# Two-layer decoder trunk in fp32 on one core: work reordered at the second mixer's entry and behind the last expert, the last gate product cut in two, decay logits in rounded parts

## The chip, the core and the metric

The kernel runs on one core of one Trainium2 chip. The metric is device time in microseconds of one execution. The engines are TensorE (PE), VectorE (DVE), ScalarE (ACT), GpSimd (POOL) and SyncE (SP); each works through its own instructions in order, and waits on semaphores tie them together.

## What is computed

A causal decoder trunk of two layers on 256 tokens of width 1024, all fp32:

```
for i in range(2):
    u = rmsnorm(h, mix_norm_gain[i])
    fq, fk, fv, fg, hq, hf, hi, hg = split(u @ w_in[i])
    a = head_rmsnorm(forgetting_attention(fq, fk, fv, fg, bias[i]))
    r = head_rmsnorm(hgrn2_recurrence(hq, hf, hi, lower_bounds[i])) * silu(hg)
    h = h + concat(a, r) @ w_out[i]
    u = rmsnorm(h, ffn_norm_gain[i])
    h = h + (swiglu(u) if i == 0 else moe_swiglu(u))      # top 2 of 8 experts
    u = rmsnorm(h, ple_norm_gain[i])
    h = h + (p[i] @ w_ple[i]) * sigmoid(u @ w_ple_gate[i])
return rmsnorm(h, final_norm_gain)
```

The attention's logits are `q.k * scale + c[q] - c[k]` with `c` the running sum of the log forget gates; the softmax cancels `c[q]`.

## The kernel before

**Split products.** A weight chunk is 1 MB (128 x 2048 numbers in fp32). SP loads it into one of 7 `raw` slots as soon as PE has consumed the chunk 7 before. ACT rounds it to fp32r (`whi`, 6 slots, L580 in the static part and L588 in the expert part), VectorE subtracts (`wlo`, in the raw slot, L907). The activations are split likewise into `uTh` (ACT, L595, or L816 in the last norm) and `uTl` (VectorE, L973 or L1436). A product is three matmuls (`product`, L1507 to L1511): `uTh.whi`, `uTh.wlo`, `uTl.whi`. A quarter is one tile of 128 tokens, 512 output columns and half of the 8 blocks of depth: 12 matmuls. Most products stream 512 columns of weights; the transposed projections stream 256 columns of `uTh`.

**Order by hand.** Each engine's order is written out. `hi_upto(n)` and `hi(n, i)` place ACT's roundings of weights, `lo_upto(n)` and `lo(n, i)` VectorE's subtractions. A norm of tile t is: sum of squares and root on ACT (`norm`, L564), small operations and the scaled tile `un` on VectorE (L940, with gains L947), eight transposes on PE (L1504), an eviction with gains on VectorE (L965), rounding on ACT and subtraction on VectorE. Functions of different tables on ACT need a table load (`preload_act_table`).

**Second mixer's entry.** Layer 0 ends with its gate product (`gated`, L1812): four quarters for tile 0, then four for tile 1, with the transposes of norm 3's tile 0 after the third (`turn_next`, L1826). VectorE adds the gated embedding half by half (`add_ple`, L1229); on ACT and VectorE the split of weight chunk `pe0 + 6` (second half of `hg`) stands ahead of tile 0's rounding and gains (L796 to L798, L1322 to L1324). Then `mixer(1)` begins: PE computes `hg` for tile 0, waits for a bank (L1733), computes `forget` for tile 0 (the forget gates' logits, plain fp32, L1577), transposes norm 3's tile 1 (L1736), and computes `hg` and `forget` of tile 1.

**Logits.** `pair_logits` (L1614) adds `-c[k]` to each head's `q.k` with an fp32 matmul of a selector `pick` with `negc`, on 64 rows for each head, the two halves of the array in turn; 128 columns for tile 0, 256 for tile 1. `negc` comes from VectorE (L1072).

**Experts and tail.** The tokens of each expert form items of up to 128; here there are 8. ACT and PE run all items in a loop. VectorE runs the last one in a copy of its own (L1470). Each item has 42 chunks (`EXP_LOADS`), split 4 ahead (`LEAD`), so that in the last item ACT also rounds the tail's chunks 0 to 3 (embedding weights, then gate weights) before it evicts the item's result `y` to `ysb` (`y_out`, L823). PE spreads `ysb` over the tokens (L2038), VectorE adds the other items' results, read back from memory (L1413, L1414), and then these (L1427). Norm 5 and layer 1's gate product follow (`gated(1)`), tile 0's four quarters and tile 1's. For tile t the end is: two sigmoids (L719), product and sum (L1233, L1234), square and root (L566, L568), small operations, one multiplication of 1024 columns with the root and the final gain (L1490), one store of 512 KB from SP (L456).

## Time and profile before

| | us |
|---|---|
| median of 3 runs | 1558.0 (1557.21 to 1559.49) |
| the profiled execution, its own time | 1561.19 |
| its span in the profile | 1559.4 |
| PE busy in it | 1525.3 (98%) |
| DVE busy | 1231.3 (79%) |
| ACT busy | 999.7 (64%) |
| POOL busy | 53.4 (3%) |
| mean granted clock of PE, share of full speed | 0.993 |
| DMA, mean over the span | 291 GB/s |

Matmul durations overlap in the profile, since matmuls are pipelined: a split product's matmul of 512 columns lasts 0.39 us there, and the next one starts some 0.23 us after it. So progress on PE is read from start to start. "Idle before" tells how long an engine stood still and what released it. An fp32 matmul counts as two in the profile.

### The profile page before, as it was taken

What the parts mean: (1) busy time and instruction counts of PE and PEld (TensorE: products, weight loads), DVE (VectorE), ACT (ScalarE), POOL (GpSimd) and SP (SyncE); (2) the same over time, 40 slices, a digit from 0 to 9 for tenths busy, and PEclk for the clock granted to TensorE, in tenths of its full rate; (3) what the DMA queues carried; (4) which work ended last, traced back from release to release, by engine and by line L of the source; (5) the groups of instructions that cost most, each with busy time, mean ns of one, the idle gap of its engine ahead of it and who ended that gap; (6) DMA issues with size and microseconds to landing.
All of it is one profiled execution on the core that took longest, in us unless ns stands there. A gap on an engine that the chain in (4) does not pass through costs nothing.

```text
span 1559.4 us, 21216 instructions
## 1 busy us (share of the span) xinstructions
PE 1525.3 (98%) x7951; PEld 1282.3 (82%) x7951; DVE 1231.3 (79%) x1090; ACT 999.7 (64%) x846; POOL 53.4 (3%) x76
## 2 busy tenths in 40 slices
PE   7999999999999999999999999999999999999987
...
GB/s 300 136 109 82 257 207 188 191 165 161 163 109 122 170 226 375 379 372 382 380 372 387 378 372 386 375 373 387 379 365 391 378 364 389 376 372 389 370 326 27
DMA packets 206641, 453.36 MB, mean 291 GB/s; under 512 B 12472, under 2 KB 31488, under 8 KB 206336
## 3 DMA queue, kind: packets, MB, share of 16 engines
...
q8 instruction: 33, 0.54, 0.1%
q14 instruction: 16, 0.13, 0.0%
...
## 4 chain that ended last, share of the span: by engine, by line
PE 92%; DVE 4%; ACT 1%; DMA 1%; issue 1%; ACTq 0%; DVEq 0%; POOL 0%; SPq 0%; POOLq 0%
PE bank L1509 28%; PE bank L1511 28%; PE bank L1510 27%; PE bank L1600 2%; PE bank L1990 2%; DVE wlo L907 1%; PE bank L1655 1%; DMA raw<-in_w_ple_gate_dram 1%; PE bank L1669 0%; PE bank L1577 0%; PE bank L1963 0%; DMA raw<-in_w_exp_gate_dram 0%; PE bank L1609 0%; DVE uTl L973 0%; PE bank L1633 0%
## 5 line engine op out<-in xcount | busy, mean ns | idle before, releaser
L907 DVE TENSOR_TENSOR wlo<-raw,whi 128x2048 fp32r<-128x2048 f32 x415 | 937.1, 2288 | 151.7 <-ACT whi L588 92.9
L588 ACT ACTIVATE whi<-raw 128x2048 fp32r<-128x2048 f32 x341 | 640.7, 1912 | 59.4 <-DMA raw<-in_w_exp_down_dram 28.5
L1509 PE MATMUL bank<-whi,uTh 128*128 128x512 f32 (+1 forms) x1304 | 515.4, 395 | 6.5 <-DVE uTl L973 4.7
L1511 PE MATMUL bank<-whi,uTl 128*128 128x512 f32 (+1 forms) x1304 | 506.8, 389 | 0.0
L1510 PE MATMUL bank<-wlo,uTh 128*128 128x512 f32 (+1 forms) x1304 | 505.8, 388 | 0.0
L1509 PEld LDWEIGHTS bank<-whi,uTh 128*128 128x128 f32 x1304 | 245.8, 189 | 57.5 <-DVE uTl L973 5.8
L1511 PEld LDWEIGHTS bank<-whi,uTl 128*128 128x128 f32 x1304 | 245.7, 188 | 51.5
L1510 PEld LDWEIGHTS bank<-wlo,uTh 128*128 128x128 f32 x1304 | 246.0, 189 | 47.5
L1509 PE MATMUL bank<-whi,hTr 128*128 128x512 f32 x528 | 207.4, 393 | 0.0
L1511 PE MATMUL bank<-whi,hTr 128*128 128x512 f32 x528 | 205.7, 390 | 0.0
L1510 PE MATMUL bank<-wlo,hTr 128*128 128x512 f32 x528 | 205.5, 389 | 0.0
L580 ACT ACTIVATE whi<-raw 128x2048 fp32r<-128x2048 f32 x74 | 138.7, 1912 | 1.0 <-DMA raw<-in_w_in_dram 0.9
L724 ACT ACTIVATE hTr<-bank 128x512 fp32r<-128x512 f32 x56 | 33.6, 599 | 143.0 <-PE bank L1990 143.0
L1511 PEld LDWEIGHTS bank<-whi,hTr 128*128 128x128 f32 x528 | 99.1, 188 | 20.9
L1509 PEld LDWEIGHTS bank<-whi,hTr 128*128 128x128 f32 x528 | 99.2, 188 | 20.6 <-issue 0.7
L1510 PEld LDWEIGHTS bank<-wlo,hTr 128*128 128x128 f32 x528 | 99.2, 188 | 20.1
L1509 PE MATMUL bank<-uTh,whi 128*128 128x256 f32 x256 | 74.1, 290 | 0.0
L1510 PE MATMUL bank<-uTl,whi 128*128 128x256 f32 x256 | 72.4, 283 | 0.0
L1511 PE MATMUL bank<-uTh,wlo 128*128 128x256 f32 x256 | 72.4, 283 | 0.0
L638 ACT ACTIVATE work<-bank 128x512 f32<-128x512 f32 x24 | 14.3, 597 | 61.3 <-PE bank L1511 61.2
L766 ACT ACTIVATE hTr<-bank 128x512 fp32r<-128x512 f32 x10 | 5.4, 596 | 74.2 <-PE bank L1845 74.2
L1509 PEld LDWEIGHTS bank<-uTh,whi 128*128 128x128 f32 x256 | 49.1, 192 | 1.2
...
## 6 DMA issues: line engine op xcount, KB each, us to landing
...
```

The lines of the kernel that those rows point to most:

```text
L580: nc.scalar.activation(whi[:, n % SPLIT, :], raw[:, n % RAW, :], ACT.Copy).then_inc(hi_a, 1)
L588: nc.scalar.activation(whi[:, s % SPLIT, :], raw[:, s % RAW, :], ACT.Copy).then_inc(hi_a, 1)
L638: nc.scalar.activation(to, b, func, scale=scale).then_inc(proj_a[l], 1)
L724: nc.scalar.activation(exhT[r % 2][0], bank(4, 4, P), ACT.Copy).then_inc(exT_hi, 1)
L766: nc.scalar.activation(ffT[0][:, t, 0:nt, :], bank(2 + t, 4, P)[:, 0:nt, :], ACT.Copy).then_inc(ffT_hi, 1)
L907: return V.tensor_tensor(wlo[:, n % RAW, :], raw[:, n % RAW, :], whi[:, n % SPLIT, :].bitcast(F32), ALU.subtract).then_inc(lo_ready, 1)
L1509: T.matmul(o, sth, mvh, start=start, stop=False)
L1510: T.matmul(o, sth, mvl, start=False, stop=False)
L1511: return T.matmul(o, stl, mvh, start=False, stop=stop)
L1600: last = T.matmul(b[:, t * NP + hp, :], keyT[r, hp, t * P:(t + 1) * P], later, start=True, stop=True)
L1655: last = T.matmul(bank(FOX_BANK[t])[:, hd * HD:(hd + 1) * HD], probsT[u][:, i * nk + kt, :], fv[:, kt, hd * HD:(hd + 1) * HD], start=kt == ...
L1990: last = T.transpose(bank(4, 4, P)[:, c, :], exh[r % 2][:, c * P:(c + 1) * P], ident[:, :])
```

## The change

- PE: the transposes of norm 3's tile 0 come after the second quarter of tile 1 instead of the third; norm 3's tile 1 is transposed before `forget` of tile 0 and before the wait for its bank; norm 5's tile 1 is transposed after the third quarter of tile 0 instead of the second.
- ACT and VectorE at that entry: tile 0's rounding, gains and first gate half come ahead of the split of chunk `pe0 + 6`.
- Logits: `pick` is rounded in place to fp32r once (ACT, layer 0), `negc` is split into a rounded part (ACT, a new wait on `negc_ready`) and a rest (VectorE) that live in the place of `fgt`. Tile 1's matmuls with `pick` become two fp32r ones each; tile 0's stays one fp32 matmul.
- ACT's last expert item becomes a copy of its own behind the loop, which rounds only the tail's chunk 0. Chunk 1 is rounded behind norm 5's tile 0, chunks 2 to 4 behind `last_hi(0)`. VectorE subtracts chunk 3 before norm 5's tile 1.
- Last half of layer 1's gate product for tile 1: instead of two quarters of 512 columns, two parts of 256 columns over the whole depth, in banks 7 and 4. Its sigmoids, products, sums and squares go by these parts, the mean of squares is gathered from three sums, the final gain is multiplied in early, and the last multiplication works in two halves, of which SP stores one and ACT the other, 256 KB each.

```diff
@@ -176,7 +176,9 @@
         ones = sb("ones", [P, SEQ])
+        pick_at = (nc.sbuf_base + 31) // 32 * 32
         pick = sb("pick", [P, NH, P])
+        pickr = nc.alloc_sbuf_tensor_at("pickr", [P, NH, P], F32R, offset=pick_at)
         wfg = sb("wfg", [P, KT, P])
@@ -186,7 +188,9 @@
         negc = sb("negc", [P, SEQ])
+        fgt_at = (nc.sbuf_base + 31) // 32 * 32
         fgt = sb("fgt", [P, 2, SEQ])
+        negr = nc.alloc_sbuf_tensor_at("negr", [P, 2, SEQ], F32R, offset=fgt_at)
         eps = sb("eps", [P, 1])
...
@@ -451,10 +458,11 @@
                         sp.dma_start(back[t], rows2.rearrange("(p k) n -> p k n", k=2)).then_inc(yb_in[t], 16)
-            for t in range(TT):
-                sp.wait_ge(out_ready, t + 1)
-                sp.dma_start(out[0, t * P:(t + 1) * P, :], fout[:, t, :]).then_inc(stored, 16)
-            sp.wait_ge(stored, 16 * TT)
+            sp.wait_ge(out_ready, 1)
+            sp.dma_start(out[0, 0:P, :], fout[:, 0, :]).then_inc(stored, 16)
+            sp.wait_ge(out_ready, 2)
+            sp.dma_start(out[0, P:2 * P, 0:NC], fout[:, 1, 0:NC]).then_inc(stored, 16)
+            sp.wait_ge(stored, 16 * (TT + 1))
@@ -660,6 +668,11 @@
                 hi_upto(first + 8)
+                if l == 0:
+                    act.wait_ge(consts, CONSTS)
+                    nc.scalar.activation(pickr[:, :, :], pick[:, :, :], ACT.Copy)
+                act.wait_ge(negc_ready[l], 1)
+                nc.scalar.activation(negr[:, 0, :], negc[:, :], ACT.Copy).then_inc(negh_ready[l], 1)
                 for j, (to, scale) in enumerate(((hqT, 1.0), (qT, HD ** -0.5), (kT, 1.0))):
@@ -793,9 +806,9 @@
             nc.scalar.preload_act_table(ACT.Sigmoid)
+            hi_parts(TURN_NORM[3], 0)
+            gate(0, 1, 0, consumed, pe0 + 3)
             hi_upto(pe0 + 6)
-            gate(0, 1, 0, consumed, pe0 + 3)
-            hi_parts(TURN_NORM[3], 0)
             gate(0, 1, 1, consumed, pe0 + 5)
@@ -846,7 +859,10 @@
             n_items = act.value_load(item_expert[0:1, ITEMS:ITEMS + 1], min_val=NE, max_val=ITEMS)
-            with act.Fori(0, n_items) as i:
+            last_item = act.value_load(item_expert[0:1, ITEMS + 1:ITEMS + 2], min_val=NE - 1, max_val=ITEMS - 1)
+            def item(i, ahead):
                 for n, (kind, r, hf) in enumerate(EXP_ORDER):
@@ -860,14 +876,22 @@
                         turn_hi(i, EXR - 1)
-                    hi(n + LEAD, i)
+                    if n + LEAD < ahead:
+                        hi(n + LEAD, i)
                 y_out(i)
+            with act.Fori(0, last_item) as i:
+                item(i, EXP_LOADS + LEAD)
+            item(last_item, EXP_LOADS + 1)
             nc.scalar.preload_act_table(ACT.Sqrt)
-            for t in range(TT):
-                act.wait_ge(hacc, 1 + t)
-                norm(5, t)
+            act.wait_ge(hacc, 1)
+            norm(5, 0)
+            hi(1, n_items)
+            act.wait_ge(hacc, 2)
+            norm(5, 1)
             last_hi(0)
-            hi(LEAD, n_items)
+            for n in range(2, LEAD + 1):
+                hi(n, n_items)
             last_hi(1)
@@ -876,11 +900,24 @@
             nc.scalar.preload_act_table(ACT.Sigmoid)
-            for n in range(2):
-                gate(1, 1, n, consumed, n_items * EXP_LOADS + (NSTATIC + 3 + 2 * n))
+            gate(1, 1, 0, consumed, n_items * EXP_LOADS + (NSTATIC + 3))
+            act.wait_ge(h_ready[6], 3)
+            nc.scalar.activation(un[:, 1, 0:NC], h[:, 1, 0:NC], ACT.Square, accum_out=ssq_part[:, 0:1]).then_inc(part_sq, 1)
+            for j, (c0, n) in enumerate(LAST_PARTS):
+                act.wait_ge(last_gate, j + 1)
+                nc.scalar.activation(sig[:, 1, c0:c0 + n], bank(LAST_GATE[j])[:, 0:n], ACT.Sigmoid).then_inc(ple_sig[1], 1)
+                if j == 0:
+                    act.wait_ge(h_ready[6], 4)
+                    nc.scalar.activation(un[:, 1, c0:c0 + n], h[:, 1, c0:c0 + n], ACT.Square, accum_out=ssq_part[:, 1:2]).then_inc(part_sq, 1)
             nc.scalar.preload_act_table(ACT.Sqrt)
-            act.wait_ge(h_ready[6], 4)
-            norm(6, 1)
+            act.wait_ge(h_ready[6], 5)
+            c0, n = LAST_PARTS[-1]
+            nc.scalar.activation(un[:, 1, c0:c0 + n], h[:, 1, c0:c0 + n], ACT.Square, accum_out=ssq[:, 1:2]).then_inc(sq_done, 1)
+            act.wait_ge(sq_done, 6 * TT + 2)
+            act.wait_ge(part_ms, 1)
+            nc.scalar.activation(ry[:, 1:2], ssq[:, 1:2], ACT.Sqrt, bias=ms_part, scale=1.0 / D).then_inc(ry_ready, 1)
+            act.wait_ge(out_ready, 3)
+            act.dma_start(out[0, P:2 * P, NC:D], fout[:, 1, NC:D]).then_inc(stored, 16)
@@ -1162,6 +1199,8 @@
                 lo_upto(first + 9)
+                dve.wait_ge(negh_ready[l], 1)
+                V.tensor_tensor(negr[:, 1, :], negc[:, :], negr[:, 0, :].bitcast(F32), ALU.subtract).then_inc(negl_ready[l], 1)
                 dve.wait_ge(proj_a[l], 6)
@@ -1319,9 +1358,9 @@
             norm(3, 0)
+            gains(TURN_NORM[3], 0, norm_rows(3))
+            add_ple(0, 1, 0)
             lo_upto(pe0 + 6)
-            add_ple(0, 1, 0)
-            gains(TURN_NORM[3], 0, norm_rows(3))
             add_ple(0, 1, 1)
@@ -1477,17 +1516,46 @@
             lo(2, n_items)
+            lo(3, n_items)
             norm_gained(5, 1, 2)
-            lo(3, n_items)
+            lo(4, n_items)
             last_rest(1)
-            lo(4, n_items)
-            for t in range(TT):
-                for n in range(2):
-                    add_ple(1, t, n)
-                norm_root(6, t)
-                link(V.tensor_tensor(ry[:, t:t + 1], ry[:, t:t + 1], rt[:, t:t + 1], ALU.mult))
-                dve.wait_ge(fgain_in, 16)
-                V.scalar_tensor_tensor(fout[:, t, :], h[:, t, :], ry[:, t:t + 1], fgain, ALU.mult, ALU.mult).then_inc(out_ready, 1)
+            for n in range(2):
+                add_ple(1, 0, n)
+            norm_root(6, 0)
+            link(V.tensor_tensor(ry[:, 0:1], ry[:, 0:1], rt[:, 0:1], ALU.mult))
+            dve.wait_ge(fgain_in, 16)
+            V.scalar_tensor_tensor(fout[:, 0, :], h[:, 0, :], ry[:, 0:1], fgain, ALU.mult, ALU.mult).then_inc(out_ready, 1)
+            def gained_out(c0, n):
+                V.tensor_tensor(fout[:, 1, c0:c0 + n], h[:, 1, c0:c0 + n], fgain[:, c0:c0 + n], ALU.mult).then_inc(dchain, 1)
+                chain[0] += 1
+            add_ple(1, 1, 0)
+            dve.wait_ge(h_ready[6], 3)
+            gained_out(0, NC)
+            for j, (c0, n) in enumerate(LAST_PARTS):
+                dve.wait_ge(ple_sig[1], 4 + j)
+                s = slice(c0, c0 + n)
+                link(V.tensor_tensor(prod[:, 1, s], bank(3)[:, c0 - NC:c0 - NC + n], sig[:, 1, s], ALU.mult))
+                V.tensor_tensor(h[:, 1, s], h[:, 1, s], prod[:, 1, s], ALU.add).then_inc(h_ready[6], 1)
+                if j == 0:
+                    dve.wait_ge(part_sq, 2)
+                    link(V.tensor_tensor(ms_part, ssq_part[:, 0:1], ssq_part[:, 1:2], ALU.add))
+                    V.tensor_scalar(ms_part, ms_part, 1.0 / D, EPS, ALU.mult, ALU.add).then_inc(part_ms, 1)
+                dve.wait_ge(h_ready[6], 4 + j)
+                gained_out(c0, n)
+            dve.wait_ge(part_ms, 1)
+            dve.wait_ge(sq_done, 6 * TT + 2)
+            link(V.tensor_scalar(ms[:, 1:2], ssq[:, 1:2], 1.0 / D, ms_part, ALU.mult, ALU.add))
+            dve.wait_ge(ry_ready, 6 * TT + 2)
+            link(V.reciprocal(ry[:, 1:2], ry[:, 1:2]))
+            link(V.scalar_tensor_tensor(rt[:, 1:2], ry[:, 1:2], ry[:, 1:2], ms[:, 1:2], ALU.mult, ALU.mult))
+            link(V.tensor_scalar(rt[:, 1:2], rt[:, 1:2], -0.5, 1.5, ALU.mult, ALU.add))
+            for c0 in (0, NC):
+                v = fout[:, 1, c0:c0 + NC]
+                V.tensor_scalar(v, v, ry[:, 1:2], rt[:, 1:2], ALU.mult, ALU.mult).then_inc(out_ready, 1)
@@ -1620,6 +1688,7 @@
                         pe.wait_ge(cross_ready[l], 2)
+                        pe.wait_ge(negl_ready[l], 1)
                     if i == 2:
@@ -1632,7 +1701,11 @@
                         for o, r, hd in both:
-                            last = T.matmul(o, pick[r, hd, :], negc[r, 0:n], start=False, stop=True)
+                            if t == 0:
+                                last = T.matmul(o, pickr[r, hd, :].bitcast(F32), negc[r, 0:n], start=False, stop=True)
+                            else:
+                                T.matmul(o, pickr[r, hd, :], negr[r, 0, 0:n], start=False, stop=False)
+                                last = T.matmul(o, pickr[r, hd, :], negr[r, 1, 0:n], start=False, stop=True)
                             if j == len(some) - 1:
@@ -1730,10 +1803,9 @@
                         if t == 0:
+                            norm(3, 1)
                             pe.wait_ge(h_ready[3], 3)
                         forget(t * P, P)
-                        if t == 0:
-                            norm(3, 1)
                 begin()
@@ -1817,12 +1889,12 @@
                         last.then_inc(first_gate[l], 1)
-                    if (n, hf) == (0, l):
+                    if (n, hf) == (l, 0):
                         norm(3 * l + 2, 1)
                 pe.wait_ge(uT_ready, ready + 4)
-                for n, hf in QUARTERS:
+                for n, hf in QUARTERS[:2] if l == 1 else QUARTERS:
                     one_tile(bank(6 + n), chunk_in(1 + 2 * n + hf), 1, hf, HALF).then_inc(consumed, 1)
-                    if (n, hf) == (1, 0):
+                    if (n, hf) == (0, 1):
                         turn_next()
@@ -2040,6 +2112,16 @@
             gated(1, tail_in, lambda: None)
+            pe.wait_ge(ple_sig[1], 1)
+            for j, (c0, n) in enumerate(LAST_PARTS):
+                for hf in range(2):
+                    wh, wl = tail_in(3 + hf)
+                    for k in range(HALF):
+                        kk = hf * HALF + k
+                        c = slice(c0 - NC, c0 - NC + n)
+                        last = product(bank(LAST_GATE[j])[:, 0:n], uTh[:, kk, P:2 * P], uTl[:, kk, P:2 * P], wh[:, k, c], wl[:, k, c],
+                                       start=kk == 0, stop=kk == KT - 1)
+                last.then_inc(last_gate, 1)
@@ -2057,6 +2139,8 @@
 TOKENS = [7, 3]
+LAST_GATE = [7, 4]
+LAST_PARTS = [(NC, NC // 2), (NC + NC // 2, NC // 2)]
 LAST_BANK = [[4, 5], [7, 6]]
```

## Rows read from the trace of the kernel before

**Rows 1.** The page's part 4: chain that ended last, shares of the span.

```profile
PE 92%; DVE 4%; ACT 1%; DMA 1%; issue 1%; ACTq 0%; DVEq 0%; POOL 0%; SPq 0%; POOLq 0%
PE bank L1509 28%; PE bank L1511 28%; PE bank L1510 27%; PE bank L1600 2%; PE bank L1990 2%; DVE wlo L907 1%; PE bank L1655 1%; DMA raw<-in_w_ple_gate_dram 1%; PE bank L1669 0%; PE bank L1577 0%; PE bank L1963 0%; DMA raw<-in_w_exp_gate_dram 0%; PE bank L1609 0%; DVE uTl L973 0%; PE bank L1633 0%
```

**Rows 2.** PE's timeline at the second mixer's entry: start, duration, line, instruction, [idle before].

```profile
374.67 1.03 PE L1504 MATMUL bank<-ident,un 128*128 128x128 f32 x8
...
379.79 0.50 PE L1509 MATMUL bank<-whi,uTh 128*128 128x512 f32 x1 [1.35 <-DVE uTl L973]
...
385.37 1.95 PE L1577 MATMUL bank<-work,wfg 128*128 128x128 f32 x16
387.15 1.04 PE L1504 MATMUL bank<-ident,un 128*128 128x128 f32 x8
390.52 0.50 PE L1509 MATMUL bank<-whi,uTh 128*128 128x512 f32 x1 [2.34 <-DVE uTl L973]
...
397.73 1.95 PE L1577 MATMUL bank<-work,wfg 128*128 128x128 f32 x16
```

**Rows 3.** Windows: stretch, its length, busy us of each engine, PEclk, DMA share, GB/s.

```profile
391.90:395.30 3.40, 3.40 (x10) 2.62 (x9) 2.30 (x2) 3.35 (x3) 0.00 (x0) 0.50 0.02 5
1514.90:1518.30 3.40, 3.40 (x5) 1.35 (x4) 1.16 (x2) 1.25 (x1) 0.00 (x0) 0.50 0.01 2
399.80:405.00 5.20, 5.20 (x45) 5.20 (x45) 2.29 (x1) 1.95 (x2) 0.00 (x0) 1.00 0.54 186
```

**Rows 4.** PE's timeline behind the last expert item.

```profile
1514.42 5.40 PE L2038 MATMUL bank<-work 128*128 128x512 f32 x8 [4.16 <-ACT work L823]
...
1536.65 0.50 PE L1509 MATMUL bank<-whi,uTh 128*128 128x512 f32 x1 [1.04 <-DVE wlo L907]
```

**Rows 5.** The end: timelines of ACT and VectorE, and the output's DMA issues.

```profile
1550.58 0.60 ACT L719 ACTIVATE work<-bank 128x512 f32<-128x512 f32 x1 [4.84 <-PE bank L1511]
1552.66 1.06 ACT L566 ACTIVATE un<-h 128x1024 f32<-128x1024 f32 x1 [0.18 <-DVE h L1234]
1555.00 1.28 DVE L1490 SCALAR_TENSOR_TENSOR work<-h,small,work 128x1024 f32<-128x1024 f32 x1
out_dram<-work SPq DMA_DIRECT2D x2, 512.0 KB, 2.7
```

**Rows 6.** VectorE's timeline at the second mixer's entry.

```profile
370.94 0.81 DVE L940 TENSOR_SCALAR un<-h,small 128x1024 f32<-128x1024 f32 x1
...
380.38 0.69 DVE L1234 TENSOR_TENSOR h<-h,work 128x512 f32<-128x512 f32 x1
...
389.17 1.29 DVE L973 TENSOR_TENSOR uTl<-work,uTh 128x512 fp32r<-128x512 f32 x2
```

**Rows 7.** ACT's timeline at the second mixer's entry.

```profile
370.28 1.28 ACT L795 ACT_TABLE_LOAD   x1
371.58 1.92 ACT L580 ACTIVATE whi<-raw 128x2048 fp32r<-128x2048 f32 x1
```

**Rows 8.** PE's timeline at the second tile's logits, layer 1.

```profile
478.54 0.60 PE L1633 MATMUL bank<-work 64*128 64x256 f32 x4
478.97 0.60 PE L1635 MATMUL bank<-negc,pick 64*128 64x256 f32 x4
479.50 0.50 PE L1509 MATMUL bank<-whi,uTh 128*128 128x512 f32 x1
479.84 0.40 PE L1510 MATMUL bank<-wlo,uTh 128*128 128x512 f32 x1
```

**Rows 9.** VectorE's and PE's timelines where `negc` is made, layer 1.

```profile
421.48 0.29 DVE L1072 TENSOR_SCALAR negc<-fgt 128x256 f32<-128x256 f32 x1
...
425.52 1.16 PE L1609 MATMUL bank<-work 64*128 64x128 f32 x16
```

**Rows 10.** ACT's timeline at the end of the last expert item.

```profile
1511.97 1.91 ACT L588 ACTIVATE whi<-raw 128x2048 fp32r<-128x2048 f32 x1 [0.80 <-DMA raw<-in_w_ple_gate_dram]
1513.79 1.07 ACT L823 ACTIVATE work<-bank 128x512 f32<-128x512 f32 x2
```

**Rows 11.** VectorE's timeline behind the last expert item.

```profile
1511.39 1.28 DVE L1414 SCALAR_TENSOR_TENSOR h<-work,small,h 128x1024 f32<-128x1024 f32 x1
```

3 lines of the change are left out of this document (added).

## The prediction

> **What bounds the kernel now.** I read the chain that ended last first: 92% of the span lies on TensorE (PE), and the three matmul lines of the split products alone carry most of it [rows 1]. So an edit counts only where PE stands still, runs slowly, or issues other work. Next I read PE's timeline for waits where the change acts. At the entry of the second mixer PE waits 1.35 us for tile 0's `uTl` and 2.34 us for tile 1's [rows 2]; the windows then show 3.4 us at a granted clock of 0.50, that is 1.2 GHz, right after the second wait [rows 3]. After the last expert item PE waits 4.16 us for `ysb`, and again 3.4 us at 0.50 follow [rows 3, 4]. In the last gate it waits 1.04 us for a weight's low part [rows 4]. Behind PE's last matmul some 9 us remain in which it has no part [rows 5]. All times below are within the profiled execution's span of 1559.4 us.
>
> **Entry of the second mixer.** The norm of tile 0 is ready at 370.94 + 0.81 = 371.75. Its eight transposes start at 374.67, after gate quarter (1,0); a quarter sooner they start at 371.9 [rows 2, 6]. Tile 1 shows what they lead to undisturbed: transposes 387.15, low part 389.17 to 390.46, so 3.3 us from the first transpose to the end [rows 2, 6]. ACT's rounding now comes ahead of the 1.92 us weight split that starts at 371.58 [rows 7]; tile 0's `uTl` is then ready at 375.3, well ahead of PE's end of the gate at 379.79 - 1.35 = 378.4. The whole 1.35 goes. The displaced split ends near 376.9 and its low part (2.3 us on VectorE) near 379.1; PE needs it with the second quarter at 381, so it is hidden. What is late next is tile 1: its last gate sigmoid falls near 378.5 to 379.1, VectorE adds the product by 380.6 instead of 380.38 + 0.69 = 381.07 [rows 6], and so its norm is ready near 383.6. PE ends tile 0's `hg` product at 378.3 + 24 matmuls x 0.227 = 383.7 (24 of them took 379.79 to 385.37 [rows 2]). Now the transposes come first (0.8), then `forget` (387.15 - 385.37 = 1.78 [rows 2]) covers part of their 3.3 us: `uTl` at 387.0 to 387.1, where it was 390.52. The start of tile 1 moves by **-3.4**. Its 24 matmuls took 397.73 - 390.52 = 7.21, against 5.58 for tile 0's [rows 2]: the slow clock cost 1.6. I take it as gone, since the wait left is 0.8 us and the wait of 1.35 us was followed by no slow clock: **-1.6**, -5.0 in all. From there to the experts ACT and VectorE are paced by PE.
>
> **Logits.** For the second tile each layer has four groups of two fp32 `pick` products, 0.43 us a group (478.54 to 478.97), that become four fp32r ones. No row shows such a product on 64 rows. If halves of the array overlap fully, as two fp32 ones do now, a group takes two slots of 0.12, else four: 0.24 or 0.48 (0.12 is the spacing of fp32r matmuls of 256 columns, 5.20 us for 45 less the two cut at the edges [rows 3]). In the written order half of it can overlap: 0.36. Against it stand switches of type, six more a layer: leaving fp32 costs 0.10 before the next matmul starts (479.50 - 478.97 - 0.43), and 0.11 after it (479.84 - 479.50 = 0.34 against 0.23) [rows 8]; I take 0.08 for each, as the row mixes change of type and of height. Best per layer 4 x (0.24 - 0.43) = -0.76, worst 4 x 0.05 + 6 x 0.2 = +1.4, taken -0.28 + 0.48 = +0.2; two layers **+0.4**, ends -1.5 and +2.8. The new waits: ACT stands for `negc`, ready at 421.48 + 0.29; queued behind it are the first eviction of `hq` (0.6), a split of 1.9 and the second eviction, which PE's first level waits for. By my count this ends at 425.1 and PE asks at 425.52 [rows 9]: hidden, slack 0.4, and what overruns is paid in full. In layer 0 ACT also rounds `pick` (1 us, as half a weight chunk's 1.91); the eviction comes 2.8 later, and PE next needs one 5 us on. VectorE's extra subtraction (0.4) precedes work that waits for PE anyway. The extra register load before the loop falls where ACT is ahead of PE: nothing; bounded by one microsecond.
>
> **End of the last item.** ACT splits three gate chunks, each waiting for its DMA, the last 1511.97 to 1513.88, and only then evicts `y` at 1513.79 [rows 10]. PE had ended at 1514.42 - 4.16 = 1510.26 [rows 4]. With the splits behind it, `y` starts at 1510.35 and PE's slot products at 1511.0. They took 4.8 us, 3.4 of it at half clock [rows 3]; at full clock 3.1 to 3.4, so they end near 1514.5. VectorE ends adding the gathered experts at 1511.39 + 1.28 = 1512.67 [rows 11] and is next late: the four additions end near 1515.7 instead of 1520.5: **-4.8**. Tile 0's transposes follow at 1517.85.
> Now the splits of chunks 1 to 4 (1.92 each) stand among the norms. ACT: 1517.35, then norm and rounding of tile 0 to 1519.85, then 1521.75, 1523.65, 1525.5. VectorE's low parts end near 1519.75, 1524.0, 1526.2 and 1530.5. PE asks for them at 1521.7, 1524.4, 1527.1 and 1530.6: hidden, by 0.1 to 2 us. The 1.04 us wait goes (**-1.0**), since tile 1's norm now comes ahead of the fourth chunk and its transposes after the third quarter. Last half of the gate: 48 matmuls of 256 columns x 0.12 = 5.76 for 24 x 0.227 = 5.44: **+0.3**. PE ends 5.5 earlier.
>
> **Behind the last matmul.** Now: sigmoid at 1550.58, product, sum, square over 1024 columns (1.06), root, small operations, one multiplication of 1.28 from 1555.00, and 3.1 us to the end, 2.7 of them the store of 512 KB [rows 5]. New, from PE's end: sigmoid 0.4, product 0.4, sum 0.45 on 256 columns; the Sqrt table load (1.28) starts behind the sigmoid and ends 0.4 after the sum; square 0.6, root 0.35, small ones 0.65, two halves of 0.45. That is 4.5 for 5.9, by one count: **-1.4**. The two half stores have separate queues; the second moves half the bytes, worth between 0 and 1.3: **-0.7**. Together **-2.1**.
> Rows show a table load of 1.28 us from 370.28 and the next ACTIVATE at 371.58, with nothing between [rows 7]. The Trainium skill (ScalarE: Activation LUTs, What `ACT_TABLE_LOAD` costs) adds a drain of about 1.38 us to each switch; by it the end would come 1.4 us later, about 1547.2. The trace disagrees with it here, and the sum goes by the row.
>
> **Sum**: -5.0 + 0.4 - 4.8 - 1.0 + 0.3 - 2.1 = -12.2 us. The profiled execution's own time, 1561.19, lies 1.8 above its span and 3.2 above the median of 1558.0; taken off the median the forecast is 1545.8 us.
>
> **Rivals.**
> 1. The slow clock stays or comes back at both places (the waits left are near 0.8 us; after 1.35 us the clock held, after 2.34 and 4.16 it fell). Entry +1.6; at the tail the slot products cost 1.7 more, of which VectorE's additions hide 0.6. Together 2.7: 1548.5. Chance 0.17.
> 2. The fp32r logits cost their bad end, each switch 0.2 and no overlap: 2.8 instead of 0.4: 1548.2. For it: the row at 479.50. Chance 0.13.
> 3. The entry's gain is given back among the experts, whose loads fill the DMA engines while ACT waits for them. Then 12.2 - 5.0 = 7.2 is left: 1550.8. Against it: each load is released by PE's own consumption, so its start moves too. Chance 0.08.
> 4. Slower: ACT's last item is no longer in the loop but in its own copy, 42 chunks long; should fetching it stall ACT, PE runs dry once the four chunks split ahead are used, 4 x 2.7 less the 4.2 that split and low part take: about 6.7 us. Only beyond 6.7 does it cost; beyond 6.7 + 12.2 + 3.1 = 22.0 us the kernel is slower than measurable. VectorE makes the same step from loop to copy today with no such gap. A stall of 23 us gives 1558.0 - 12.2 + 16.3 = 1562. Chance 0.02.
> The forecast has 0.60.
>
> A difference of 0.2% (3.1 us) is what a measurement here can tell. The forecast and rivals 1 to 3 all lie beyond it; several misses together could leave the kernel within it (0.03). Faster 0.95, same 0.03, slower 0.02. Range: from the good end of the logits (1.9 less), the store's full 1.3 (0.6 less) and additions that end with VectorE's own count (four of 0.62 behind 1512.67, 0.4 less), together 1542.9, to rival 3: **1542.9 to 1550.8**.
>
> **What would show it.** Right: tile 0's `hg` starts with no wait and tile 1's near 387.1; windows of granted clock 0.50 are absent behind 387 and behind the slot products; ACT's `y` starts within 0.2 us of PE's last expert matmul; no PE wait in the last gate; 4 to 5 us from the last matmul to the last multiplication. Wrong: a PE wait at the second mixer's first level (the `negc` wait showed through), `pick` groups longer than 0.43, waits for `wlo` at the last gate's quarters, or a store as long as before.

## The result, and the profile after

The changed kernel takes **1545.65 us** (median of 4 runs, 1543.96 to 1546.96); beside it on the same chip the kernel before took 1557.95 (1557.21 to 1559.49). The ratio is 0.9913, with an interval of 0.9902 to 0.9925. A later set gave 1546.91 against 1560.41 and a ratio of 0.9910 (0.9895 to 0.9925). So the change is worth 13.5 to 14 us by the ratios and 12.3 by the medians of the first set; the forecast was 12.2 and 1545.8 us. The profiled execution's own time is 1546.96 us, its span 1545.2, against 1561.19 and 1559.4.

At the second mixer's entry, PE's timeline in the profile after (start, duration, line, instruction, idle before) answers to [rows 2]:

```profile
371.18 1.04 PE L1572 MATMUL bank<-ident,un 128*128 128x128 f32 x8
...
382.99 1.03 PE L1572 MATMUL bank<-ident,un 128*128 128x128 f32 x8
383.86 1.95 PE L1645 MATMUL bank<-work,wfg 128*128 128x128 f32 x16
386.35 0.50 PE L1577 MATMUL bank<-whi,uTh 128*128 128x512 f32 x1 [0.55 <-DVE uTl L1010]
...
391.94 1.95 PE L1645 MATMUL bank<-work,wfg 128*128 128x128 f32 x16
```

The wait of 1.35 us ahead of tile 0's `hg` is gone, the one of 2.34 is 0.55, and tile 1's 24 matmuls take 391.94 - 386.35 = 5.59 us instead of 7.21. Behind the last expert item, the first rows are ACT's timeline, the next two PE's, and the last three VectorE's ([rows 4, 10, 11] before):

```profile
1503.97 1.09 ACT L836 ACTIVATE work<-bank 128x512 f32<-128x512 f32 x2 [5.87 <-PE bank L1579]
1505.08 1.28 ACT L886 ACT_TABLE_LOAD   x1
...
1504.62 3.70 PE L2110 MATMUL bank<-work 128*128 128x512 f32 x8 [0.77 <-ACT work L836]
1507.76 0.79 PE L1577 MATMUL bank<-whi,pT 128*128 128x512 f32 x1
...
1505.00 1.28 DVE L1453 SCALAR_TENSOR_TENSOR h<-work,small,h 128x1024 f32<-128x1024 f32 x1
1506.32 1.89 DVE L1466 TENSOR_TENSOR h<-bank,h 128x512 f32<-128x512 f32 x3
1508.36 0.69 DVE L1466 TENSOR_TENSOR h<-bank,h 128x512 f32<-128x512 f32 x1 [0.15 <-PE bank L2110]
```

ACT stands waiting for PE when the item ends, instead of PE for ACT. The slot products take 3.70 us for 5.40 by their records (from first to last, ends included), and VectorE, not PE, is now late: three of its four additions follow each other without a gap. The windows (stretch, its length, busy us of each engine, PEclk, which is the granted clock, DMA share, GB/s) show the clock, at the places of [rows 3] and in the router:

```profile
386.30:389.70 3.40, 3.35 (x15) 2.77 (x16) 0.87 (x1) 3.39 (x3) 0.00 (x0) 1.00 0.02 5
533.10:543.30 10.20, 10.20 (x50) 10.20 (x51) 2.99 (x20) 1.41 (x4) 0.10 (x1) 0.50 0.19 74
563.80:567.20 3.40, 3.40 (x10) 2.72 (x9) 2.94 (x3) 2.40 (x2) 0.00 (x0) 0.50 0.63 243
1504.60:1508.00 3.40, 3.38 (x9) 1.63 (x9) 3.33 (x5) 2.10 (x3) 0.00 (x0) 1.00 0.70 257
```

Both stretches at 0.50 (1.2 GHz) that the forecast wanted gone are gone. In the router one of 10.2 us stands, where the profile before had 6.8 (542.1 to 548.9). The end, ACT's, VectorE's and PE's timelines mixed by start, then the DMA issues ([rows 5] before):

```profile
1537.87 0.28 PE L1579 MATMUL bank<-whi,uTl 128*128 128x256 f32 x1
1538.19 0.38 ACT L908 ACTIVATE work<-bank 128x256 f32<-128x256 f32 x1 [1.03 <-PE bank L1579]
1538.59 1.28 ACT L912 ACT_TABLE_LOAD   x1
...
1539.88 0.42 ACT L915 ACTIVATE un<-h 128x256 f32<-128x256 f32 x1
...
1541.46 1.00 DVE L1558 TENSOR_SCALAR work<-work,small 128x512 f32<-128x512 f32 x2
...
out_dram<-work SPq DMA_DIRECT2D x1, 256.0 KB, 2.1
out_dram<-work ACTq DMA_DIRECT2D x1, 256.0 KB, 2.3
```

From the last matmul's start to the span's end it is 7.33 us, where it was 9.24 (1559.4 - 1550.16).

To see where time went, cut each profile at six starts on PE: **A** from the span's start to tile 1's `forget` (391.94 above, 397.73 in [rows 2]); **A-B** on to the transposes of tile 1's router norm; **B** the router, on to the first item's transposes at the wait of 2 us for VectorE; **C** the experts, on to the slot products; **D** on to tile 0's last transposes; **E** on to the last matmul; **F** to the end. The lengths, each the difference of two rows of PE's timeline:

| profile | A | A-B | B | C | D | E | F | span |
|---|---|---|---|---|---|---|---|---|
| before | 397.73 | 137.82 | 33.17 | 945.70 | 8.27 | 27.47 | 9.24 | 1559.4 |
| after | 391.94 | 137.04 | 34.37 | 941.27 | 6.70 | 26.55 | 7.33 | 1545.2 |
| difference | -5.79 | -0.78 | +1.20 | -4.43 | -1.57 | -0.92 | -1.91 | -14.2 |

A holds the entry and layer 0's logits, A-B layer 1's logits; C ends with the wait for `ysb` (4.16 before, 0.77 after). B has no edit in it. What is left of C beside that wait is -1.0; the only edits there are ACT's extra register load and its copy of the last item.

### The profile page after: what moved, and what is told of

It is laid out like the page before. It is cut to its first block, busy times and chain, and to the rows that moved or that the text cites. A ratio compares the mean times of both kernels' runs of the same rounds, so it can differ in the third digit from the quotient of the medians.

```text
span 1545.2 us, 21285 instructions
## 1 busy us (share of the span) xinstructions
PE 1521.4 (98%) x7975; PEld 1283.8 (83%) x7975; DVE 1233.1 (80%) x1099; ACT 997.1 (65%) x852; POOL 53.5 (3%) x76
## 4 chain that ended last, share of the span: by engine, by line
PE 95%; DVE 3%; ACT 1%; issue 0%; DMA 0%; ACTq 0%; DVEq 0%; POOL 0%; POOLq 0%
PE bank L1577 29%; PE bank L1579 28%; PE bank L1578 28%; PE bank L1668 2%; PE bank L2062 2%; DVE wlo L944 1%; PE bank L1728 1%; PE bank L1572 0%; PE bank L1742 0%; PE bank L2035 0%; PE bank L1677 0%; PE bank L1702 0%; DMA rows<-in_hgrn_lb_logits_dram 0%; PE bank L2044 0%; PE bank L1717 0%
```

## The experiments

Ten are the changed kernel, alone, with one part undone or, in one, with more filler; two are the kernel before, one of them with filler. Nothing is left out of the computation in any. Single runs of one kernel differ by 3 us and more, and its medians moved by 1.3 us (after: 1545.65, 1546.91) and 2.5 us (before: 1557.95, 1560.41), as much as most parts are worth. So the verdicts rest on the lengths above, one profile of each kernel; those of all twelve (F uses a span given to 0.1 us, so it is good to 0.05):

| profile | A | A-B | B | C | D | E | F | median, runs |
|---|---|---|---|---|---|---|---|---|
| b_before | 397.49 | 137.81 | 32.72 | 944.08 | 8.78 | 27.48 | 9.24 | 1559.64 |
| b_fill | 396.10 | 137.81 | 32.74 | 944.25 | 8.27 | 27.49 | 9.24 | 1558.05 |
| a_after | 392.09 | 137.05 | 34.37 | 943.14 | 6.70 | 26.56 | 7.29 | 1546.91 |
| u_logits | 393.49 | 137.84 | 32.72 | 940.95 | 6.69 | 26.55 | 7.36 | 1548.27 |
| u_entry | 395.24 | 137.06 | 31.55 | 939.81 | 6.71 | 26.54 | 7.29 | 1550.11 |
| u_entry2 | 395.29 | 137.03 | 34.37 | 942.12 | 6.68 | 26.56 | 7.35 | 1551.01 |
| u_forget | 395.29 | 137.05 | 33.16 | 941.22 | 6.71 | 26.53 | 7.34 | 1548.92 |
| u_item | 391.91 | 137.05 | 34.37 | 944.56 | 8.27 | 26.54 | 7.30 | 1551.28 |
| u_norm5 | 391.91 | 137.06 | 33.18 | 941.34 | 6.70 | 27.88 | 7.33 | 1546.51 |
| u_end | 391.87 | 137.01 | 31.54 | 939.67 | 6.71 | 26.11 | 9.19 | 1545.39 |
| u_store | 391.95 | 137.05 | 33.17 | 942.61 | 6.69 | 26.56 | 7.67 | 1547.51 |
| r_warm | 391.91 | 137.07 | 33.09 | 942.26 | 6.71 | 26.55 | 7.31 | 1545.63 |

Read down a column: an edit moves its own part, and the others repeat within 0.2 us. B and C are the exception, since they move in kernels that are alike there. Two values stand out besides: A of `u_logits`, which starts late (below), and D of `b_before`, 8.78 for the 8.27 of `before`: there the granted clock is at 0.50 for 6.8 us, from 2.3 us ahead of the slot products, where `before` has 3.4.

### u_logits: the logits with one fp32 matmul again

```diff
-                            if t == 0:
-                                last = T.matmul(o, pickr[r, hd, :].bitcast(F32), negc[r, 0:n], start=False, stop=True)
-                            else:
-                                T.matmul(o, pickr[r, hd, :], negr[r, 0, 0:n], start=False, stop=False)
-                                last = T.matmul(o, pickr[r, hd, :], negr[r, 1, 0:n], start=False, stop=True)
+                            last = T.matmul(o, pickr[r, hd, :].bitcast(F32), negc[r, 0:n], start=False, stop=True)
```

> The changed kernel, but tile 1's logits use the one fp32 pick matmul again; the splitting of negc on ACT and VectorE stays. The two traces place the gain at 0.79 us a layer. Theory A: the fp32r matmuls of the two row halves overlap fully (a group of two heads 0.24 us for 0.43) and a switch between fp32r and fp32 costs nothing of its own. Then the groups are 0.96 to 0.97 us apart again instead of 0.77, each layer is 0.8 us longer, both 1.6, and the time is about 1547.2 us. Rival B, the term of my forecast (half overlap, 0.08 us for each switch): the logits got 0.2 us a layer slower by the change, the 0.8 comes from elsewhere, and this kernel is 0.4 us faster than the changed one. Rival C: the new form changes nothing by itself: 0 and groups of 0.77 as they are.

Measured: 1548.27 us, ratio 0.9927 (0.9914 to 0.9941); A-B +0.80, A +1.55 (0.8 of it logits, the rest a later start: PE's `forget` of layer 0, which comes ahead of any logits, starts at 38.51 instead of 37.70, and all behind it with it). PE's timeline of one stretch of layer 0, first after, then this kernel:

```profile
108.46 0.60 PE L1702 MATMUL bank<-work 64*128 64x256 f32 x4
108.70 0.47 PE L1707 MATMUL bank<-negr,pickr 64*128 64x256 f32 x2
109.01 0.28 PE L1708 MATMUL bank<-negr,pickr 64*128 64x256 f32 x2
109.22 0.50 PE L1577 MATMUL bank<-whi,uTh 128*128 128x512 f32 x1
```

```profile
109.47 0.60 PE L1702 MATMUL bank<-work 64*128 64x256 f32 x4
109.90 0.60 PE L1704 MATMUL bank<-negc,pickr 64*128 64x256 f32 x4
110.43 0.50 PE L1577 MATMUL bank<-whi,uTh 128*128 128x512 f32 x1
```

From the queries to the first weight matmul behind it: 0.76 us in the one, 0.96 in the other. With 0.43 for the queries and 0.10 that both pay at the exit, the two heads' `pick` products take 0.23 instead of 0.43. That is two slots of 0.12, so the halves of the array overlap fully and the switches of type inside add nothing that a row shows. Theory A holds, B and C fall.

### u_entry, u_entry2: the old order at the entry

```diff
-            hi_parts(TURN_NORM[3], 0)
-            gate(0, 1, 0, consumed, pe0 + 3)
             hi_upto(pe0 + 6)
+            gate(0, 1, 0, consumed, pe0 + 3)
+            hi_parts(TURN_NORM[3], 0)
...
-            gains(TURN_NORM[3], 0, norm_rows(3))
-            add_ple(0, 1, 0)
             lo_upto(pe0 + 6)
+            add_ple(0, 1, 0)
+            gains(TURN_NORM[3], 0, norm_rows(3))
...
-                            norm(3, 1)
                             pe.wait_ge(h_ready[3], 3)
                         forget(t * P, P)
+                        if t == 0:
+                            norm(3, 1)
...
-                    if (n, hf) == (0, 1):
+                    if (n, hf) == (1, 0):
                         turn_next()
```

> The changed kernel, with the order of the second mixer's entry as it was before on PE, ACT and VectorE. Theory A: the order there gives 5.0 us, 3.4 from the waits and 1.6 from the 3.4-us stretch at half clock behind them. Then the two waits (1.35 and 2.34 us) and the half clock behind the second are back, and the time is about 1550.6 us. Rival B: what the entry gives is taken back among the experts, whose loads hold ACT: the entry is 5 us later, the start of the last stage is not, and the time is 1545.6 to 1546.5. Rival C: the half clock has no part in it: 3.4 us more, 1549.0. It also shows whether the stretch at half clock in the router, 10.2 us in the changed kernel and 6.8 before, hangs on the time at which the entry passes: if so it is 6.8 again and gives 1.2 us back, so 1549.4.

> The variant with the old entry order once more, for a second profile and more times. Its first five times were 1546.0 and 1546.8 us at a mean granted clock of 0.998 and 1550.1 to 1551.4 at 0.995 and 0.996. Theory A: the 3.4-us stretch of 0.50 behind the 2.34-us wait comes in some executions and not in others, as the stretches of the router do; the waits of 1.35 and 2.34 us stand in each, and the times fall into the same two groups. Rival B: it came only with the surroundings of the kernel before, so this profile has none behind the wait again and the two groups differ by the router alone.

Measured: 1550.11 us (1546.03 to 1551.37), ratio 0.9936 (0.9922 to 0.9949); again, 1551.01, ratio 0.9949 (0.9934 to 0.9964). A is +3.30 and +3.35. Both waits are back in both profiles, yet behind the second the clock holds; PE's timeline and the window of the first:

```profile
378.94 0.50 PE L1577 MATMUL bank<-whi,uTh 128*128 128x512 f32 x1 [1.35 <-DVE uTl L1010]
...
389.67 0.50 PE L1577 MATMUL bank<-whi,uTh 128*128 128x512 f32 x1 [2.33 <-DVE uTl L1010]
```

```profile
389.70:393.10 3.40, 3.40 (x15) 2.83 (x16) 0.95 (x1) 3.39 (x3) 0.00 (x0) 1.00 0.02 5
```

So the order gives 3.3 us in both (A's part of waits), and in these two profiles no clock came with it: theory A's 1.6 us for the clock are not borne out here. B, the rival that the gain is given back in the experts, falls: C is 939.81 and 942.12, and of the kernels with the new order the one with the same router, B, has 939.67 (`u_end`) beside the first, and 941.27 and 943.14 (both profiles of after) beside the second. The medians are 3.2 to 5.4 us up. In the second set, all four runs lie in the upper group, with a granted clock of 0.994 to 0.995, although its profile shows no stretch at 0.50 at the entry: the upper group is made by the router and the experts there (B 34.37, C 942.12, against 31.55 and 939.81), and theory A of the second run, that the entry's stretch makes the groups, isn't borne out.

### u_forget: tile 1's transposes behind `forget` again, PE alone

```diff
                         if t == 0:
-                            norm(3, 1)
                             pe.wait_ge(h_ready[3], 3)
                         forget(t * P, P)
+                        if t == 0:
+                            norm(3, 1)
```

> The changed kernel with tile 1's transposes behind forget again, on PE alone; ACT and VectorE keep the new order, and tile 0's transposes stay a quarter sooner. Theory A: the transposes ahead of forget let its 1.78 us cover part of the 3.3 us from transposes to uTl. Moved back, PE waits 2.3 to 2.4 us for tile 1's uTl where it waits 0.55 now: 1.8 us more, 1547.5, and 1.6 more in executions where the clock falls behind the longer wait. Rival B: VectorE's earlier norm is what shortened the wait, and PE's order is worth less than 1 us. The waits of the entry then divide: 1.35 for tile 0's place and the rest for this one.

Measured: 1548.92 us, ratio 0.9932 (0.9918 to 0.9945); A +3.35. PE's timeline and the window behind the wait:

```profile
388.13 0.68 PE L1577 MATMUL bank<-whi,uTh 128*128 128x512 f32 x1 [2.33 <-DVE uTl L1010]
```

```profile
388.30:391.70 3.40, 3.40 (x9) 2.63 (x10) 1.09 (x1) 3.39 (x3) 0.00 (x0) 0.50 0.02 5
```

The wait is 2.33 for 0.55, the start 388.13 for 386.35: 1.78 us, to the hundredth what `forget` takes. The other 1.57 is what the 3.4 us at 0.50 behind it cost. Theory A. The entry's 3.3 us of waits are so divided into 1.8 for this place and 1.5 for the rest of the new order.

### b_fill, b_before: is it idleness that slows the clock?

`b_fill` is the kernel before with this behind tile 1's `norm(3, 1)`:

```diff
                         if t == 0:
                             norm(3, 1)
+                            for _ in range(20):
+                                T.transpose(bank(3)[:, 0:P], ident[:, :], ident[:, :])
```

> The kernel before with one edit: 20 transposes into an unused bank behind tile 1's norm at the second mixer's entry, which fill 2.2 us of the 2.34 us wait for uTl. The wait stays, only PE isn't idle in it. Theory A: PE's idleness there brings the 3.4-us stretch of 0.50 behind it, and filling takes it away: 24 matmuls in 5.58 us instead of 7.21, 1.6 us less than before, ratio 0.9990. Rival B: the stretch comes from something else, or comes and goes by chance (in the variant with the old entry order both waits were there and the clock held): no difference beyond the scatter. Rival C: the filler holds PE beyond the wait: up to 0.3 us more.

> The kernel before once more, for a second profile. Theory A: the waits and the starts between the stretches of slow clock repeat within 0.1 us, while the stretches themselves come by chance: the one at 392 to 395 may be missing, the router may show 3.4 to 13.6 us. Rival B: before's stretch at 392 and its 6.8 us in the router come again, since the wait ahead of them is the same each time. Its time is 1557 to 1561 in either case. The experts' stretch up to the slot products may differ by up to 2 us, as the four profiles of one router show (941.3 to 943.1 us between the same two landmarks).

Measured: `b_fill` 1558.05 us, ratio 0.9991 (0.9979 to 1.0002), so its median alone settles nothing; A is 396.10, which is 1.63 less than in `before` and 1.39 less than in `b_before`. `b_before` 1559.64, ratio 1.0003 (0.9993 to 1.0012). PE's timeline of `b_fill`, then the window behind its wait, then the window of the stretch in `b_before`:

```profile
388.02 2.35 PE L1738 MATMUL bank<-ident 128*128 128x128 f32 x20
390.52 0.50 PE L1509 MATMUL bank<-whi,uTh 128*128 128x512 f32 x1 [0.16 <-DVE uTl L973]
...
396.10 1.95 PE L1577 MATMUL bank<-work,wfg 128*128 128x128 f32 x16
```

```profile
390.50:393.90 3.40, 3.38 (x15) 2.81 (x16) 0.90 (x1) 3.39 (x3) 0.00 (x0) 1.00 0.00 0
```

```profile
390.20:393.60 3.40, 3.15 (x7) 2.48 (x8) 0.87 (x2) 3.39 (x3) 0.00 (x0) 0.50 0.02 5
```

With the filler the start stands at 390.52 as before, and no stretch at 0.50 follows; unfilled, the kernel before had one twice of two. But the variants of one and the same wait of 2.33 to 2.34 us, unfilled, had it in three profiles of five (`before`, `b_before`, `u_forget`; not in `u_entry` and `u_entry2`), so one profile of `b_fill` can't show that the filler did it. What is shown: when the stretch comes it costs 1.5 to 1.6 us (tile 1's 24 matmuls take 7.21 in `before`, 7.04 in `b_before` and 7.16 in `u_forget`, for 5.58), and it never came behind the wait of 0.55 (eight profiles). Its start isn't tied to the instructions: it begins at 391.9 in `before` and at 390.2 in `b_before`, there 0.3 us before the wait ends, and the instructions of the two lie 0.1 us apart.

### a_after: the changed kernel again

> The changed kernel once more, unaltered, beside the others on this chip: it gives a second profile of it. In its first profile PE's granted clock stood at 0.50 for 10.2 us in the router and 3.4 us near 564; the four variants, whose router is the same, show 10.2, 6.8, 3.4 and 3.4 us there. Theory A: these stretches differ from one execution to the next by themselves, and the 1.2 us that the first profile seemed to give back in the router is chance: this profile may show 3.4 to 13.6 us of 0.50 there, and the runs scatter by some 3 us with the mean granted clock, while the waits and the starts between them repeat within 0.1 us. Rival B: the change made the stretch longer: 10.2 us at 533 to 543 again, and the runs scatter no more than those of before. Time either way 1544 to 1547.

Measured: 1546.91 us (1546.5 to 1549.01), ratio 0.9910. B is 34.37 again, with the stretch of 10.2 us again, C 943.14 against 941.27. Taken alone this speaks for rival B there. But no kernel except `r_warm` edits the router, and windows of 0.2 us give the same picture for all fourteen profiles: B is 31.5 with one stretch of 3.4 us at 0.50 that begins 6.6 to 6.8 us behind the transposes (`u_entry`, `u_end`), 32.7 with one of 6.8 that begins 4.6 to 5.1 behind them (`u_logits`, `b_before`, `b_fill`), 33.1 to 33.2 with one of 6.8 that begins 5.9 to 6.6 behind them (`before`, `u_forget`, `u_norm5`, `u_store`, `r_warm`), and 34.4 with one of 10.2 that begins 3.7 to 4.2 behind them (both profiles of after, `u_item`, `u_entry2`). So it comes at a different place in the same instructions, and its length and cost go with the place; what sets the place isn't shown. One and the same kernel has two of these, 31.55 and 34.37 (`u_entry`, `u_entry2`), so they come by execution: theory A. The last two groups have one more stretch of 3.4 us, at the start of C (563.8 in the window above). With the new tail C is 939.67 to 940.95 without that second stretch and 941.22 to 943.14 with it, and 1.5 us apart also in the kernel before (944.08 and 944.25, against 945.70). On top of that come waits now and then: in the profile with 943.14 PE waits three times, 1.1 us in all, for VectorE's additions at L1497, in that with 941.27 not once.

### r_warm: more filler in the router

```diff
-            warm(14)
+            warm(20)
             norm(MOE_NORM, 1)
...
-            warm(4)
+            warm(13)
             scores_of(1)
```

> The changed kernel with longer filler in the router: 20 instead of 14 transposes ahead of tile 1's norm and 13 instead of 4 ahead of its scores, so that PE's waits of 0.74 and 1.07 us there are filled (0.108 us each). Theory A: PE's thin use there brings the stretches of 0.50, each 3.4 us of which costs 1.3 to 1.7 us; with it filled, at most one of them stays: about 1.5 to 4 us less than the changed kernel, 1542 to 1544, and runs that scatter less. Rival B: the filler changes nothing, since the stretches come with the small matmuls behind it (8 columns and 128 columns of fp32): within 0.5 us of the changed kernel. Rival C: the filler overruns the waits: up to 0.4 us more.

Measured: 1545.63 us, ratio 0.9902 (0.9887 to 0.9917), which the interval doesn't tell from the changed kernel's 0.9910. Its windows of 0.2 us have 0.50 from 534.9 to 541.7 and from 562.2 to 565.6, as `u_norm5` and `u_store` without the filler have (6.8 and 3.4 us), and B is 33.09 against 33.17. The filler covers the waits of 0.74 and 1.07 us (0.18 of another comes up) and the stretches come all the same. That speaks for rival B, as far as one profile goes; what makes them come isn't shown. It was meant as a version that beats both kernels, and isn't one.

### u_item: ACT's last item in the loop again

```diff
-            last_item = act.value_load(item_expert[0:1, ITEMS + 1:ITEMS + 2], min_val=NE - 1, max_val=ITEMS - 1)
...
-            with act.Fori(0, last_item) as i:
+            with act.Fori(0, n_items) as i:
                 item(i, EXP_LOADS + LEAD)
-            item(last_item, EXP_LOADS + 1)
...
-            hi(1, n_items)
...
-            for n in range(2, LEAD + 1):
-                hi(n, n_items)
+            hi(LEAD, n_items)
```

> The changed kernel with ACT's last item inside the loop again, so that the tail's chunks 1 to 3 are split ahead of the eviction of y as before; the order of PE and VectorE in the tail stays the changed one. Theory A: the eviction is what kept PE waiting. PE waits 4.2 us for ysb again and runs at half clock behind it, the norms start 4.8 to 5.0 us later, and the time is about 1550.5 us. Rival B: the order of norms and chunks made the gain, not the eviction: PE waits 4 us for ysb but only what is not hidden by VectorE's additions comes through, under 1 us: 1546.5. Rival C: the half clock does not come back with the wait: 3.4 us more, 1549.0.

Measured: 1551.28 us (1550.6 to 1551.78), ratio 0.9945 (0.9931 to 0.9959). ACT's timeline, then PE's, then the window:

```profile
1505.44 1.91 ACT L596 ACTIVATE whi<-raw 128x2048 fp32r<-128x2048 f32 x1 [0.81 <-DMA raw<-in_w_ple_gate_dram]
1507.25 1.07 ACT L836 ACTIVATE work<-bank 128x512 f32<-128x512 f32 x2
```

```profile
1507.89 5.40 PE L2106 MATMUL bank<-work 128*128 128x512 f32 x8 [3.94 <-ACT work L836]
...
1516.16 1.09 PE L1568 MATMUL bank<-ident,un 128*128 128x128 f32 x8
```

```profile
1509.10:1512.50 3.40, 3.40 (x5) 1.35 (x4) 1.67 (x3) 1.76 (x4) 0.00 (x0) 0.51 0.01 2
```

The wait is 3.17 us longer (3.94 for 0.77) and D 1.57 (8.27 for 6.70): 4.7, and with the same router as after the span is 4.8 longer. Theory A in every part, the slow clock too; the time is 0.8 above its 1550.5.

### u_norm5: the last norm where it was

```diff
-            lo(3, n_items)
             norm_gained(5, 1, 2)
-            lo(4, n_items)
+            lo(3, n_items)
             last_rest(1)
+            lo(4, n_items)
...
-                    if (n, hf) == (l, 0):
+                    if (n, hf) == (0, l):
                         norm(3 * l + 2, 1)
```

> The changed kernel with the last norm of tile 1 where it was: PE transposes it behind gate quarter (0,1), and VectorE takes it ahead of the low part of chunk 3, whose successor again waits behind last_rest(1). Theory A: this placement alone made the wait of 1.04 us for wlo in the last gate; the wait is back, about 1.0 us more, 1546.6. Rival B: the wait came from the late splits on ACT, which are now spread among the norms, and the order does nothing: 0.

Measured: 1546.51 us, ratio 0.9907 (0.9892 to 0.9922); E +1.33. The waits, in PE's timeline:

```profile
1520.59 0.50 PE L1577 MATMUL bank<-whi,uTh 128*128 128x512 f32 x1 [0.22 <-DVE wlo L944]
...
1523.22 0.39 PE L1579 MATMUL bank<-whi,uTl 128*128 128x512 f32 x1
1524.14 0.50 PE L1577 MATMUL bank<-whi,uTh 128*128 128x512 f32 x1 [0.54 <-DVE wlo L944]
1524.48 0.39 PE L1578 MATMUL bank<-wlo,uTh 128*128 128x512 f32 x1
```

The order makes the waits (theory A), in two pieces now that ACT splits later. By their records they are 0.76 us of the 1.33. The rest comes of how a wait is recorded: idle time counts from the modelled end of the matmul before, 0.39 us behind its start, while in a row of such matmuls the next one starts after 0.23. So from start to start the second wait costs 1524.14 - 1523.22 - 0.23 = 0.69, and the matmul behind it starts 0.34 later instead of 0.23: 0.80 for a recorded 0.54. The first stands right behind the transposes. From their start to the next product's it is 1.25 us there (1519.34 to 1520.59) and 0.79 in the profile after (1523.19 to 1523.98), so it costs 0.46. Together that is 1.26 of the 1.33. The wait that the kernel before has in this gate reads the same way:

```profile
1535.22 0.39 PE L1511 MATMUL bank<-whi,uTl 128*128 128x512 f32 x1
1536.65 0.50 PE L1509 MATMUL bank<-whi,uTh 128*128 128x512 f32 x1 [1.04 <-DVE wlo L907]
1536.98 0.39 PE L1510 MATMUL bank<-wlo,uTh 128*128 128x512 f32 x1
```

1.43 - 0.23 and 0.33 - 0.23 make 1.30 for a recorded 1.04. Rival B falls.

### u_end, u_store: the old end, and one store alone

Of `u_end`'s edit only parts of ACT's are shown; on SP, VectorE and PE too the end is that of the kernel before.

```diff
-            for j, (c0, n) in enumerate(LAST_PARTS):
-                act.wait_ge(last_gate, j + 1)
-                nc.scalar.activation(sig[:, 1, c0:c0 + n], bank(LAST_GATE[j])[:, 0:n], ACT.Sigmoid).then_inc(ple_sig[1], 1)
...
+            for n in range(2):
+                gate(1, 1, n, consumed, n_items * EXP_LOADS + (NSTATIC + 3 + 2 * n))
...
+            norm(6, 1)
```

and, for `u_store`:

```diff
-            sp.wait_ge(out_ready, 2)
-            sp.dma_start(out[0, P:2 * P, 0:NC], fout[:, 1, 0:NC]).then_inc(stored, 16)
+            sp.wait_ge(out_ready, 3)
+            sp.dma_start(out[0, P:2 * P, :], fout[:, 1, :]).then_inc(stored, 16)
...
-            act.wait_ge(out_ready, 3)
-            act.dma_start(out[0, P:2 * P, NC:D], fout[:, 1, NC:D]).then_inc(stored, 16)
```

> The changed kernel with the old end of the second tile: the last half of the gate in quarters of 512 columns, one square over 1024 columns, one last multiplication and one store of 512 KB. Theory A: the split end saves 1.9 us behind PE's last matmul (9.24 before, 7.33 after) and costs 0.3 to 0.5 us of PE for 48 matmuls of 256 columns in place of 24 of 512. The time is 1.5 us more, about 1547.1, with 9.2 us behind the last matmul. Rival B: 256 columns cost PE more than 0.3 us (each fp32r matmul a fixed part besides its columns): the gate ends a microsecond earlier here and the two kernels are alike, 1545.6 to 1546. Rival C: the stores of 256 KB save nothing, only the chain does: 1.1 us more, 1546.7.

> The changed kernel with one store of 512 KB for the second tile, issued by SP when both halves are multiplied, in place of two of 256 KB on SP's and ACT's queues. Behind PE's last matmul the changed kernel has 7.33 us and the variant with the whole old end 9.19. Theory A (my two terms, 1.4 chain and 0.7 store): 0.5 to 0.7 us longer behind the last matmul, 7.8 to 8.0 us. Rival B: the store's length hardly hangs on its size (the rows show 2.1 to 2.3 us for 256 KB and 2.7 for 512 KB), and the split is worth 0.4 or less: up to 7.7. Rival C: the split store costs, since two queues run side by side: 7.3 or less. In the medians none of this can be told; the trace decides.

Measured: `u_end` 1545.39 us, ratio 0.9909 (0.9894 to 0.9924); E -0.44, F +1.86. By the median, for which 1547.1 was expected, the split end is worth nothing; by the parts it is worth 1.4 us. The profile shows what can hide it: a router of 31.54 and experts of 939.67, together 4.4 us under those of after, in a span of 1542.1. Of the other three runs there is no profile, so the 1.4 us rest on the parts alone. `u_store` 1547.51, ratio 0.9915 (0.9901 to 0.9929); F +0.34. The last rows of VectorE and the store in `u_store`, and those of `u_end`:

```profile
1541.63 1.00 DVE L1556 TENSOR_SCALAR work<-work,small 128x512 f32<-128x512 f32 x2
...
out_dram<-work SPq DMA_DIRECT2D x2, 512.0 KB, 2.7
```

```profile
1532.91 0.39 PE L1536 MATMUL bank<-whi,uTl 128*128 128x512 f32 x1
...
1537.76 1.28 DVE L1515 SCALAR_TENSOR_TENSOR work<-h,small,work 128x1024 f32<-128x1024 f32 x1
```

The store's split gives 0.34 (to 0.05), the chain 1.86 - 0.34 = 1.52, and the halves cost PE 0.44. For `u_end` the parts are theory A's, the total isn't; for `u_store` it is rival B: a store of half the bytes lands after 2.1 to 2.3 us instead of 2.7.

## Why the prediction was right, step by step

| term | predicted | measured, by |
|---|---|---|
| entry: waits | -3.4 | -3.3 (`u_entry`) |
| entry: clock | -1.6 | -1.5 to -1.6 when it comes (`before`, `b_before`, `u_forget`); in three of five profiles |
| logits, both layers | +0.4 | -1.6 (`u_logits`) |
| end of the last item | -4.8 | -4.7 (`u_item`) |
| last gate: wait | -1.0 | -1.3 (`u_norm5`) |
| last gate: halves | +0.3 | +0.4 (`u_end`) |
| behind the last matmul | -2.1 | -1.9 (`u_end`), 1.5 of it chain and 0.3 store |

With the clock at -1.6, the measured terms come to -14.0, the forecast to -12.2. The ratios (0.9913, 0.9910) say -13.5 to -14.0; the median of the first set says -12.3, and the two pairs of profiles differ by -14.2 (first) and 1547.2 - 1557.6 = -10.4 (second), since the router and the experts move by some 3 us each between executions. That the forecast of the total came within 0.2 us of the first median is therefore luck: a term that was wrong by 2.0 lay inside the scatter.

**The entry.** Tile 0's low part was forecast for 375.3; in the profile after it ends at 373.21 + 1.29 = 374.5, 0.8 earlier, as everything there is by layer 0's logits. The first wait went entirely, the second start was forecast at 387.0 to 387.1 and came at 386.35 + 0.8 = 387.1 on the old clock. The waiting part followed from rows. The clock's part did not: no row of one profile says how often the stretch comes, and I took it as certain.

**The logits** are the step that failed: "in the written order half of it can overlap: 0.36. Against it stand switches of type, six more a layer ... I take 0.08 for each". Measured, both parts are their good ends: the overlap is full, 0.23 to 0.24 us a group, and the switches between fp32 and fp32r on 64 rows cost nothing that shows. The 0.10 of [rows 8] belongs to the exit to 128 rows, which both kernels have once a pair. My "best per layer" of -0.76 was the truth (-0.79). The row at 479.50 mixed two changes, and the value was taken between the ends without a row for it.

**The last item.** The chain was as forecast: ACT starts within 0.2 us of PE's last matmul (forecast 1510.35, on the old clock), and VectorE is late next. My 4.8 and 3.1 to 3.4 for the slot products were counted from their start to the next product's, while the 5.40 of [rows 4] and the 3.70 after run to their own end. In the forecast's count they take 4.83 before (1514.42 to 1519.25 in PE's timeline) and 3.14 after (1504.62 to 1507.76): as forecast, at its better end. The four additions end 2.73 us behind the first one's start, where I had about 3. **The last gate**: none of the four `wlo` waits stands in it, and the low parts were hidden as counted; the order is worth 0.3 more than the 1.04 us that the profile before records, since I took the recorded idle time for the cost of the wait, which from start to start is 1.30 (`u_norm5`). **The end**: the chain was 0.1 better, the store 0.4 worse than taken. The table load followed by an ACTIVATE 0.01 us behind its end (1538.59 + 1.28, then 1539.88) is the second such row of this case; the ACTIVATE ahead of it ends at 1538.57, 0.02 us before the load. By that the drain of about 1.38 us, which the Trainium skill (ScalarE: Activation LUTs, What `ACT_TABLE_LOAD` costs) adds to each switch, is not seen here either, and the sum was right to go by the row.

**The waits that the change adds** cost nothing: in both profiles after PE stands nowhere at the levels; ACT takes `negc` at 416.01, 0.04 us behind its end at 415.68 + 0.29.

**Rivals.** 1 (the slow clock stays): not at either place in the two profiles after; but behind the longer waits it comes in three profiles of five at the entry and in all four of the tail (`before`, `b_before`, `b_fill`, `u_item`). 2 (bad end of the logits): falls, by 4.4 us on the other side of the sum. 3 (given back among the experts): falls by `u_entry`. 4 (a stall in fetching ACT's own copy): ACT waits for PE, not the reverse, when the item ends; no stall of PE in the last item.

**Not foreseen**: that the router and the experts alone scatter by 3 us between executions. They have no edit and so no term, but the range was made of terms alone and left this scatter out.
